# Norm before the last MLP: one weight chunk's low part made in two halves, and another order of sums, squares and blocks on VectorE and ScalarE

## What is computed

```
x = x + g_a * hybrid_mixer(h, ...)            # ends with merged @ w_out
h = rms_norm(x, g_ffn[l]) * (1.0 + sc_f) + sh_f
x = x + g_f * swiglu(h, w_gate, w_up, w_down)  # (silu(h @ w_gate) * (h @ w_up)) @ w_down
return rms_norm(x, g_final)
```

## Time and profile before

| | |
|---|---|
| median of 3 runs | 976.54 us (975.61 to 976.59) |
| profiled execution: its time | 976.02 us |
| profiled execution: its span | 974.2 us |
| TensorE busy | 98% of the span |
| VectorE busy | 70% |
| ScalarE busy | 53% |
| GpSimd busy | 6% |
| mean HBM traffic | 205 GB/s |

### The profile page before, as it was taken

How to read it: one execution, slowest core, us unless ns; L and a number is a source line. 1 busy time by engine, 2 the same in 40 slices (tenths; PEclk the granted TensorE clock), 3 DMA queues, 4 the chain that set the end, 5 groups by cost and what they waited for, 6 DMA issues and landing times.

```text
span 974.2 us, 13041 instructions
## 1 busy us (share of the span) xinstructions
PE 958.3 (98%) x5134; PEld 821.6 (84%) x5134; DVE 685.5 (70%) x857; ACT 520.3 (53%) x736; POOL 57.3 (6%) x93
## 2 busy tenths in 40 slices
PE   9999999999999999999999999999999999999996
PEld 8889888888888888888888888887988788888885
DVE  6955668658887766975888877558667775656555
ACT  6666453526655555254375555537566475454443
POOL 0000131001000002100100000002100000000000
PEclk9999999999999999999999999999999999999999
DMA  9965274547988876193398898652631646555521
GB/s 324 349 203 173 88 250 151 204 130 242 316 288 298 292 270 216 45 345 92 125 343 300 290 312 288 208 168 90 224 120 54 216 148 218 191 180 193 177 82 43
DMA packets 109563, 200.89 MB, mean 206 GB/s; under 512 B 4108, under 2 KB 76060, under 8 KB 106304
## 3 DMA queue, kind: packets, MB, share of 16 engines
q1 hardware_dynamic: 106656, 189.65, 57.9%
q0 software_dynamic: 2704, 10.16, 3.1%
q10 hardware_dynamic: 144, 0.26, 0.1%
HBM read 199.00 MB, written 1.05 MB: 205 GB/s over the span
## 4 chain that ended last, share of the span: by engine, by line
PE 90%; DVE 6%; ACT 1%; issue 1%; DMA 1%; POOL 1%; POOLq 0%; SPq 0%; DVEq 0%; ACTq 0%
PE WB L355 20%; PE YB L377 10%; PE YB L381 10%; PE WB L358 10%; PE YB L372 10%; PE YB L419 5%; PE WB L372 2%; PE WB L377 2%; PE WB L381 2%; PE WB L337 2%; PE WB L344 2%; PE WB L340 2%; PE WB L698 1%; PE WB L679 1%; PE WB L457 1%
## 5 line engine op out<-in xcount | busy, mean ns | idle before, releaser
L1721 DVE TENSOR_TENSOR wl<-raw,wh 128x2048 fp32r<-128x2048 f32 (+1 forms) x150 | 343.1, 2295 | 126.7 <-ACT wh L1108 124.5
L1108 ACT CAST wh<-raw 128x2048 fp32r<-128x2048 f32 (+1 forms) x150 | 285.1, 1904 | 31.5 <-PE YB L381 9.0
L355 PE MATMUL WB<-XS,wh 128*128 128x512 f32 x832 | 208.2, 392 | 0.0
L355 PEld LDWEIGHTS WB<-XS,wh 128*128 128x128 f32 x832 | 152.2, 188 | 29.0
L358 PEld LDWEIGHTS WB<-XS,wl 128*128 128x128 f32 x832 | 113.5, 190 | 8.2
L358 PE MATMUL WB<-XS,wl 128*128 128x256 f32 x832 | 116.0, 282 | 0.0
L372 PE MATMUL YB<-wh,FHT 128*128 128x512 f32 x360 | 111.8, 392 | 0.0
L377 PE MATMUL YB<-wl,FHT 128*128 128x512 f32 x360 | 111.2, 390 | 0.0
L381 PE MATMUL YB<-wh,FLT 128*128 128x512 f32 x360 | 111.0, 389 | 0.0
L1282 ACT COPY U<-WB 128x256 f32<-128x256 f32 x102 | 33.0, 376 | 134.6 <-PE WB L358 134.6
L377 PEld LDWEIGHTS YB<-wl,FHT 128*128 128x128 f32 x360 | 67.6, 188 | 14.5
(11 more groups left out here) (335 smaller groups left out, 1219.7 us busy)
## 6 DMA issues: line engine op xcount, KB each, us to landing
raw<-in_mlp_w SPq DMA_DIRECT2D x64, 1024.0 KB, 5.2
raw<-in_w_ada SPq DMA_DIRECT2D x24, 1024.0 KB, 5.1
raw<-in_mlstm_w_in SPq DMA_DIRECT2D x11, 1024.0 KB, 7.7
raw<-in_w_ffn_down SPq DMA_DIRECT2D x11, 1024.0 KB, 5.0
raw<-in_w_ffn_gate SPq DMA_DIRECT2D x10, 1024.0 KB, 5.4
raw<-in_w_ffn_up SPq DMA_DIRECT2D x10, 1024.0 KB, 5.5
raw<-in_mem_w_kv SPq DMA_DIRECT2D x8, 1024.0 KB, 5.1
raw<-in_xattn_wq SPq DMA_DIRECT2D x8, 1024.0 KB, 6.8
```

The lines of the kernel that those rows point to most:

```text
L355: e.matmul(W[:, :], H[:, at(k)], XS[:, k, :], start=k == 0, stop=False)
L1108: f = e.copy(w[:, 0:a * b], raw[:, 0:a * b])
L1721: f = e.tensor_tensor(L[:, 0:a * b], raw[:, 0:a * b], H[:, 0:a * b].bitcast(F32), ALU.subtract)
```

## The change

VectorE no longer makes the whole low part of `("up", 0)` ahead of the gated sums. A new function `up_low(h)` makes it in two halves of 128x1024: the first after the two sums of t = 0, the second after the two sums of t = 1. `gated(1, 1)` moves ahead of the low parts of the blocks (0,0) and (0,1), and the four low parts of t = 0 now stand together behind the second half. On ScalarE the squares of (1, 0) and (1, 1) no longer stand together behind the three blocks of t = 0: the first stands behind block (0,0), the second still behind (0,3). TensorE, POOL and the order of SP's loads are unchanged.

```diff
-            def ffn_half(t):
-                for h in range(2):
-                    e.wait_ge(*dve_mix["gated", t, h])
-                    rms_half("ffn", t, h)
+            def ffn_square(t, h):
+                e.wait_ge(*dve_mix["gated", t, h])
+                rms_half("ffn", t, h)
 
             def ffn_between():
-                ffn_half(1)
-                hi_to(M["wout2", 3] + 3)
-
-            ffn_half(0)
-            norm("ffn", lambda k: MC[:, 24 + k:25 + k], lambda k: MC[:, 16 + k:17 + k], ffn_between)
+                ffn_square(1, 1)
+                hi_to(M["gate", 1])
+
+            ffn_square(0, 0)
+            ffn_square(0, 1)
+            norm("ffn", lambda k: MC[:, 24 + k:25 + k], lambda k: MC[:, 16 + k:17 + k], ffn_between,
+                 lambda: ffn_square(1, 0))
...
-            lo_to(M["wout2", 1] + 3)
-            rms_turn("ffn", lambda t, h: gated("wout2", dve_mix, 0, t, h), lambda t, h: rms_z("ffn", t, h),
-                      lambda k: MC[:, 24 + k:25 + k], lambda k: MC[:, 16 + k:17 + k])
-            lo_to(M["wout2", 3] + 3)
+            def up_low(h):
+
+                n, m, cs = N["up", 0], M["up", 0], slice(1024 * h, 1024 * h + 1024)
+                e.wait_ge(*w_hi[m])
+                f = e.tensor_tensor(WL[m % NS][:, cs], RAW[n % NR][:, cs], WH[m % NS][:, cs].bitcast(F32), ALU.subtract)
+                if h == 1:
+                    f.then_inc(w_lo.add(m))
+                    at[:] = [n + 1, m + 1]
+
+            g, b = lambda k: MC[:, 24 + k:25 + k], lambda k: MC[:, 16 + k:17 + k]
+            lo_to(M["gate", 0])
+            gated("wout2", dve_mix, 0, 0, 0)
+            gated("wout2", dve_mix, 0, 0, 1)
+            up_low(0)
+            rms_z("ffn", 0, 0)
+            rms_z("ffn", 0, 1)
+            gated("wout2", dve_mix, 0, 1, 0)
+            evac("ffn", 0, 1, g, b)
+            gated("wout2", dve_mix, 0, 1, 1)
+            up_low(1)
+            for q in range(4):
+                rms_low("ffn", 0, q)
+            rms_z("ffn", 1, 0)
+            rms_z("ffn", 1, 1)
+            evac("ffn", 1, 1, g, b)
+            evac("ffn", 1, 3, g, b)
+            for q in range(4):
+                rms_low("ffn", 1, q)
+            lo_to(M["gate", 1])
```

More of the change, by code:

```diff
@@ L1915, in rms_low @@
                                 ).then_inc(dve_ln.add(("lo", s, t, q)))
[L1917 to L1934, removed]
             class Norm:
```

## The result

| | before | changed |
|---|---|---|
| median | 976.0 us (7 runs, 975.61 to 976.83) | 973.22 us (7 runs, 972.87 to 974.06) |
| ratio to before | 1 | 0.997, 95% interval 0.9958 to 0.9982 |
| span of the profiled execution | 974.2 us | 971.8 us |
| wait of TensorE at this norm | 2.25 us | 0.19 us |

What follows compares the result with a forecast made beforehand. TensorE, 98% busy, was taken as the bound, losing time to a 2.25 us norm wait and a clock fall. 2.1 + 1.4 = 3.5 us off 976.02 gave 972.5, and a median 0.5 higher: 973.0 us, range 971.9 to 974.7.

Steps and rivals of the forecast that it cites:

- The cause: VectorE late with the first sum by one low part: At the RMS norm: VectorE's first gated sum 2.5 us late, 2.2 us of it from the second chunk's low part.
- The idle, 2.1 us won: TensorE's wait ahead of the norm's first transposes falls from 2.25 us to some 0.15.
- The first half: VectorE's 128x1024 subtraction ahead of the scaling of t = 0: 1.2 us, covered with 0.7 us left.
- POOL's row: POOL's first instruction for t = 0, 0.30 us alone, is held 0.1 us by VectorE's first piece.
- The stretch behind the first transposes, 1.4 us won: TensorE from first transposes to first part of t = 1: 9.0 us in place of 10.44, at full clock.
- the first rival: Another name for the clock rival.
- the third block: Its cast, done at 781.3, makes TensorE wait 0.1 us in the third part.
- the scaling of t = 1: Second norm on VectorE: scaling at 783.15, costing TensorE 0.05 us ahead of its transposes, 0.8 by the upper bound.
- The second half, in the fourth part: VectorE's later piece of the low part: hidden with 0.1 to 0.2 us of cover; upper bound 0.9 us wait.
- The clock rival: The clock's share of the gain isn't there: 1.0 to 1.6 us less won, 974.0 to 974.6 us; chance 0.2.
- The load of `("gate", 2)`: Issued at about 781.7 instead of 773.66, with 7 us of cover left; rival that it lands late: chance 0.03.
- the clock would not fall after the short idle: At this norm TensorE's granted clock stays at 1.00 from 776 to 786, after under 0.3 us of idle.

Runs made afterwards that it cites:

- the order alone: Changed kernel, but the whole low part of the second chunk again in front of the sums; sums and squares in the new order: 976.0 us, ratio 0.9997 to before.
- the move alone: Changed kernel with only the low part moved in halves; sum (1, 1) and both squares of t = 1 placed as before: 973.63 us, ratio 0.9976 to before.
- the half in front: Changed kernel with the first half of the low part in front of the gated sums: 974.76 us, ratio 0.9983 to before.
- ScalarE's old order: Changed kernel with both squares of t = 1 behind the third block on ScalarE, as before: 974.26 us, ratio 0.9983 to before.

## Why the prediction was right

**The cause: VectorE late with the first sum by one low part.** Right. The order alone left the time as it was, the move alone gave 0.24 of the 0.30%, and the half in front gave half of the wait back.

**The idle, 2.1 us won.** Right. 2.25 to 0.19 us, 2.06. The first half took 1.22 us against 1.2, and POOL's row 0.44 us, 0.14 more than alone against 0.1.

**The stretch behind the first transposes, 1.4 us won.** The term was mis-sized, and it mixed two things. It measured 10.44 - (786.73 - 777.41) = 1.12 us. The order alone, whose clock stayed up, needs 788.81 - 779.84 = 8.97 us for it, 1.47 under before's 10.44. By the first rival's working the clock is 1.0 of these and the order the rest; that fits ScalarE's old order, which costs 0.4 us of the stretch when the clock is up. No profile of before with the clock up was had, so this split is argued and not shown. Two waits of the changed kernel I had put too low: the third block, 0.23 against 0.1, and the scaling of t = 1. The first is in the order alone too (its third part takes 785.17 - 784.01 = 1.16 us). The second is not, and makes up 0.29 of the 0.35 us by which the changed kernel is slower here than the order alone. That scaling came 784.32 - 782.02 (the square's start) = 2.30 us after its square; I took 783.15 - 781.2 = 1.95, between 1.8 and 2.7, and TensorE lost 0.29 by it in place of 0.05. The cause is the hold of POOL by the moved low parts, as its row shows (0.76 us, 0.50 with two of them out of the way). The second half, in the fourth part, was hidden as said.

**The clock rival.** Half right. I had priced it from one profile as if every execution had the fall; by the mean clock at most some 46 of 59 have it. In the stretch 3.18 us are won with the fall in before, 0.3 less than the 3.5 forecast, by the new waits. If the fall costs 1.0 of these and 13 of 59 executions are without it, the mean gain is an estimated 3.18 - 1.0 x 13/59 = 3.0 us, and the medians differ by 2.8 and 3.1. What a fall costs is itself not settled: 1.0 us by the working, but between the executions of before at 0.998 and those at 0.996 only 0.45, and between the former and all 46 at 0.996 or 0.997 only 0.17 (976.20 and 976.37). The median came out within 0.2 us of the forecast by luck: the gain was 0.7 us smaller than forecast (2.8 against 3.5), and before's median, at 976.54 from three executions when I predicted, was 976.0 from seven. That the clock would not fall after the short idle held in both profiles of the changed kernel.

**The load of `("gate", 2)`** was issued at 782.5 and cost nothing: no wait of TensorE stands behind the norm. **What was won stayed won**: from the first matmul of t = 1 to the first of `("gate", 1)` it is 792.27 - 786.73 = 5.54 us in the changed kernel and 794.67 - 789.11 = 5.56 in before, and no wait of TensorE follows in either.

## What to carry to other kernels

When the busiest engine waits for a norm, look at what stands ahead of the norm's first step in the queue of the engine that makes it, and move bulk work that is due later into the gap where that engine itself waits, cut so that it fits the gap. Check the cut against every engine that works in that gap: here the first of POOL's two small instructions is held by VectorE's large one, so that one piece of 2.3 us in the gap costs 0.7 us more than two of 1.2. One piece behind the second sums comes too late for TensorE instead, and costs 0.5 us. And find out in how many executions a clock fall is there before pricing it from one profile. The mean clock of each execution is a first hint, and a second profile is needed, because the mean doesn't tell where the clock fell.

## What the runs showed of the hardware

- **The clock.** An idle of 2.25 us of TensorE between full stretches of work was followed, 1.0 and 1.4 us after work began again, by 3.4 us at 1.2 GHz in two profiles of before, and by none in a third kernel with the same idle. Idles of 1.19, 1.26, 1.61 and 1.78 us in the middle of the program lowered nothing in the profiles. Near the start, behind the first 3.5 to 3.8 us of work, one of 1.27 us was followed by 3.4 us at the low level (the half in front). One of 1.50 us at the same place, in the second profile of the changed kernel, was followed by none. At the end of the program the clock fell in every profile, 2 to 5 us behind the last matmul. An idle of 5.06 us lowered the clock in its profile while it lasted, and the low level then held through the first 5.5 us of work.
- **POOL behind VectorE.** POOL's one-column instruction ended 0.17 us after a single long subtraction. With four short ones in a row behind each other (0.33 us from start to start, worked out from 1.43 us for four) it did not get in at the end of the one that ran at its start (783.18) but after the next (783.51, POOL's end 783.60). With a long one and short ones behind it, it ended 0.1 us after the first short one (784.49; VectorE's long one ended at 784.07). So a row of short instructions holds POOL longer than the one that runs, but not to the end of the row.
- **The spread of executions** can come in part from POOL-issued loads of a norm's rows: the wait of VectorE for the bias at one norm was 0.72 us in one profile, 0.15 to 0.6 in ten and not seen in three, and TensorE's wait behind it 1.2 to 1.8 us.
